# A one-core float32 kernel: loads at the start reordered, and the products of the first unit rearranged

## The reference, cut to what matters

```
xn   = rms_norm(x, gain)          # x: 256 x 2048; the row factor is 1/sqrt(mean(x*x)+eps)
proj = xn @ w_in                  # dv, fv, fg, dq, dk, fq, fk are column blocks of it
```

## Time and profile before

| what | value |
|---|---|
| median of 3 runs | 2824.51 us |
| the profiled execution | 2823.42 us, span 2821.6 us |
| TensorE busy | 2788.0 us, 99% of the span |
| VectorE / ScalarE / GpSimd busy | 65% / 50% / 24% |
| first product of TensorE starts at | 8.11 us |
| DMA, mean over the span | 198 GB/s |

### The profile page before, as it was taken

How to read it: one execution, slowest core, us unless ns; L and a number is a source line. 1 busy time by engine, 2 the same in 40 slices (tenths; PEclk the granted TensorE clock), 3 DMA queues, 4 the chain that set the end, 5 groups by cost and what they waited for, 6 DMA issues and landing times.

```text
span 2821.6 us, 39092 instructions
## 1 busy us (share of the span) xinstructions
PE 2788.0 (99%) x14972; PEld 2399.4 (85%) x14972; DVE 1824.2 (65%) x2904; ACT 1409.0 (50%) x1991; POOL 689.5 (24%) x365
## 2 busy tenths in 40 slices
PE   8999999999999999999999999999999999999998
PEld 6888888888888888888888888888888888999886
DVE  5566766877777755555555555656777876555554
ACT  5454644455555544454444444446655555444454
POOL 0000000388888888800000000001201111000000
PEclk9999999999999999999999999999999999999999
DMA  7653479877777777777677777765664556666664
GB/s 258 209 163 120 130 245 317 246 191 188 192 189 189 191 188 190 191 217 223 209 223 211 225 233 223 238 208 187 187 185 153 161 153 193 186 189 189 186 195 155
DMA packets 199018, 559.02 MB, mean 198 GB/s; under 512 B 53344, under 2 KB 69872, under 8 KB 195888
## 3 DMA queue, kind: packets, MB, share of 16 engines
q1 hardware_dynamic: 161456, 554.99, 63.5%
q0 software_dynamic: 36944, 0.41, 2.8%
q10 hardware_dynamic: 432, 1.12, 0.1%
HBM read 535.32 MB, written 21.12 MB: 197 GB/s over the span
## 4 chain that ended last, share of the span: by engine, by line
PE 92%; DVE 3%; ACT 2%; DMA 1%; issue 1%; POOL 0%; DVEq 0%; ACTq 0%; SPq 0%
PE bank L530 91%; DVE wlo L906 2%; ACT whi L1621 1%; PE bank L542 1%; DMA raw<-in_w_dv 1%; DMA h_scratch<-X 0%; DMA raw<-in_w_pq 0%; DVE tmpc L909 0%; ACT EB L1621 0%; ACT L1621 0%; DVE HB L909 0%; DVE QKb L909 0%; DVE AT L1160 0%; ACT scr L1621 0%; DVE EB L968 0%
## 5 line engine op out<-in xcount | busy, mean ns | idle before, releaser
L906 DVE TENSOR_TENSOR wlo<-raw,whi 128x1024 fp32r<-128x1024 f32 (+1 forms) x965 | 1188.9, 1234 | 864.3 <-ACT whi L1621 861.2
L1621 ACT ACTIVATE whi<-raw 128x1024 fp32r<-128x1024 f32 (+1 forms) x965 | 1017.2, 1056 | 1006.5 <-PE bank L530 985.9
L530 PE MATMUL bank<-aX,whi 128*128 128x512 f32 (+1 forms) x4000 | 966.9, 391 | 0.8 <-DVE aX L941 0.8
L530 PE MATMUL bank<-whi,aX 128*128 128x512 f32 x3008 | 934.1, 390 | 9.6 <-ACT whi L1621 9.1
L530 PEld LDWEIGHTS bank<-aX,whi 128*128 128x128 f32 (+1 forms) x4000 | 728.1, 188 | 142.9 <-issue 3.0
L530 PEld LDWEIGHTS bank<-whi,aX 128*128 128x128 f32 x3008 | 565.6, 188 | 129.1 <-ACT whi L1621 9.5
L1581 POOL DMA_INDIRECT gate_scratch<-gate,place x256 | 577.4, 2255 | 261.8 <-DMA gate_scratch<-HB 183.6
L530 PE MATMUL bank<-wlo,aX 128*128 128x512 f32 x1504 | 586.9, 390 | 3.2 <-DVE wlo L906 3.2
L530 PEld LDWEIGHTS bank<-aX,wlo 128*128 128x128 f32 (+1 forms) x3984 | 513.2, 191 | 22.6 <-DVE aX L941 2.1
L530 PE MATMUL bank<-aX,wlo 128*128 128x256 f32 (+1 forms) x3984 | 530.3, 283 | 1.8 <-DVE aX L941 1.7
L530 PEld LDWEIGHTS bank<-wlo,aX 128*128 128x128 f32 x1504 | 282.8, 188 | 64.3 <-DVE wlo L906 6.5
(11 more groups left out here) (227 smaller groups left out, 1821.6 us busy)
## 6 DMA issues: line engine op xcount, KB each, us to landing
raw<-in_w_down SPq DMA_DIRECT2D x256, 512.0 KB, 3.7
raw<-in_w_up SPq DMA_DIRECT2D x256, 512.0 KB, 4.2
raw<-in_w_in SPq DMA_DIRECT2D x176, 512.0 KB, 3.7
raw<-in_w_out SPq DMA_DIRECT2D x32, 512.0 KB, 4.3
gate_scratch<-HB SPq DMA_DIRECT2D x16, 1024.0 KB, 7.5
raw<-in_w_pq SPq DMA_DIRECT2D x32, 512.0 KB, 5.7
raw<-in_w_o SPq DMA_DIRECT2D x32, 512.0 KB, 4.3
raw<-in_w_pg SPq DMA_DIRECT2D x32, 512.0 KB, 4.3
```

The lines of the kernel that those rows point to most:

```text
L530: return e.matmul(o, lhsT, rhs, start=start, stop=stop, skip_group_check=True)
L906: e.tensor_tensor(wlo[:, s, 0:n], raw[:, r, 0:n], whi[:, s, 0:n].bitcast(F32), ALU.subtract).then_inc(s_lo, 1)
L1621: return e.activation(o, i, f, **k)
```

## The change

```
-    SQ0 = 1
-    ROWS0 = G["dv", 1].first
+    SQ0 = 6
+    ROWS0 = G["dv", 1].first + 4
@@ sync (DMA issue)
         for i, (a, z) in enumerate(XT_PARTS):
             e.dma_start(xT[:, a:z, :]..., I["xT"][:, a * 256:z * 256]).then_inc(s_xt[i], 16)
-        for u in range(2, NRAW):
-            load(u)
-        e.dma_start(small ...)
-        for t in range(2):
-            e.dma_start(X[:, t, :] ...).then_inc(s_x[t], 16)
-        e.dma_start(attc ...)
-        e.dma_start(fbr ...)
+            if i < NRAW:
+                load(i)
         for u in range(NRAW, NU + NRAW + NSPL):
             load(u)
+            if u == 6:
+                e.dma_start(small ...)
+                e.dma_start(X[:, 0, :] ...).then_inc(s_x[0], 16)
+            if u == 8:
+                e.dma_start(X[:, 1, :] ...).then_inc(s_x[1], 16)
+            if u == 11:
+                e.dma_start(attc ...)
+                e.dma_start(fbr ...)
@@ tensor
+        def first_unit():
+            bs = [vacant(fill) for fill in G["dv", 0].fills]
+            for high in (True, False):
+                for kt in range(2):
+                    c = slice(kt * 512, kt * 512 + 512)
+                    if high:
+                        w.wait_ge(s_hi if kt else s_h0, 1)
+                    else:
+                        w.wait_ge(s_lo, 1)
+                    w.wait_ge(s_xh, kt + 1)
+                    for t in range(2):
+                        ts = slice(t * 128, t * 128 + 128)
+                        if high:
+                            mm(bs[t], ax_hi(kt)[:, ts], whi[:, 0, c], kt == 0, False)
+                        else:
+                            last = mm(bs[t], ax_hi(kt)[:, ts], wlo[:, 0, c], False, False)
+                    if high:
+                        w.wait_ge(s_xl, kt + 1)
+                        for t in range(2):
+                            ts = slice(t * 128, t * 128 + 128)
+                            mm(bs[t], ax_lo(kt)[:, ts], whi[:, 0, c], False, False)
+            last.then_inc(s_mm, 1)
+            tick(0)
+
+        w.wait_ge(s_one, 1)
+        for _ in range(7):
+            mm(banks[7][:, 0:256], ones[:, 0:128], ones[:, 0:256], True, True)
+        first_unit()
+        group_t("dv", 0, ax_hi, ax_lo, split_x, 1)     # 1: skips unit 0
+        group_t("dv", 1, ax_hi, ax_lo, split_x)
@@ vector
-            if kt in (1, 3, 7):
+            if kt in (1, 3, 7, 11):
                 split((kt + 1) // 4 if kt > 1 else 0)
+        def values(name, i, base):                     # the same two evacuations of a group
+            ...
+        steps(G["dv", 0])
+        for u in G["dv", 1].units:
+            step(u)
+            if u == ROWS0 + 1:
+                values("dv", 0, 1024)
+        values("dv", 1, 1024)
+        for i in range(2):
+            steps(G["fv", i])
+            values("fv", i, 0)
@@ scalar
+            if u == SQ0 - 1:
+                warm()                                 # in step(u); was before step(0)
-        for u in range(2):
-            e.dma_start(raw[:, u, :], plan.src[u]).then_inc(s_raw[u], 16)
-            if kt in (1, 3, 7):
-                split((kt + 1) // 4 if kt > 1 else 0)
-        warm()
+            if kt == 1:
+                w.wait_ge(s_raw[0], 16)
+                act(whi[:, 0, 0:512], raw[:, 0, 0:512], ACT.Copy).then_inc(s_h0, 1)
+                act(whi[:, 0, 512:1024], raw[:, 0, 512:1024], ACT.Copy).then_inc(s_hi, 1)
+            if kt in (3, 7, 11):
+                split((kt + 1) // 4)
```

More of the change, by code:

```diff
@@ L152, in _build @@
     s_raw = [sem(f"s_raw{i}") for i in range(NRAW)]
-    s_hi, s_lo, s_mm, s_half = sem("s_hi"), sem("s_lo"), sem("s_mm"), sem("s_half")
+    s_h0, s_hi, s_lo, s_mm, s_half = sem("s_h0"), sem("s_hi"), sem("s_lo"), sem("s_mm"), sem("s_half")
     s_free = [sem(f"s_free{i}") for i in range(8)]
@@ L453, in _ @@
             e.dma_start(xT[:, a:z, :].rearrange("p k c -> p (k c)"), I["xT"][:, a * 256:z * 256]).then_inc(s_xt[i], 16)
-        for u in range(2, NRAW):
-            load(u)
-        e.dma_start(small[:, :], I["small"]).then_inc(s_const, 16)
-        for t in range(2):
-            e.dma_start(X[:, t, :], I["x"][:, t * D:t * D + D]).then_inc(s_x[t], 16)
-        e.dma_start(attc[:, :], I["att"]).then_inc(s_att, 16)
-        e.dma_start(fbr[:, :], I["forget_bias"]).then_inc(s_att, 16)
+            if i < NRAW:
+                load(i)
         for u in range(NRAW, NU + NRAW + NSPL):
             load(u)
+            if u == 6:
+                e.dma_start(small[:, :], I["small"]).then_inc(s_const, 16)
+                e.dma_start(X[:, 0, :], I["x"][:, 0:D]).then_inc(s_x[0], 16)
+            if u == 8:
+                e.dma_start(X[:, 1, :], I["x"][:, D:2 * D]).then_inc(s_x[1], 16)
+            if u == 11:
+                e.dma_start(attc[:, :], I["att"]).then_inc(s_att, 16)
+                e.dma_start(fbr[:, :], I["forget_bias"]).then_inc(s_att, 16)
             now = u - NRAW - NSPL + 1
@@ L721, in group_f, with group_t @@
                 tick(u)
-        def group_t(name, i, xh, xl, ready):
+        def group_t(name, i, xh, xl, ready, skip=0):
             g = G[name, i]
             bs = [vacant(fill) for fill in g.fills]
-            for u in g.units:
+            for u in g.units[skip:]:
                 s = u % NSPL
@@ L793, in split_x @@
             w.wait_ge(s_xl, kt + 1)
-        for name in ("dv", "fv"):
-            for i in range(2):
-                group_t(name, i, ax_hi, ax_lo, split_x)
+        def first_unit():
[28 more added lines that the diff above has]
+        for i in range(2):
+            group_t("fv", i, ax_hi, ax_lo, split_x)
         g = G["fg", 0]
@@ L1254, in step @@
                     low_two("ple", kp)
-            split(u + NSPL)
+            if u:
+                split(u + NSPL)
         def finish(x):
@@ L1352, in _ @@
                                    aX[:, kt, 0:256].bitcast(F32), ALU.mult, ALU.subtract).then_inc(s_xl, 1)
-            if kt in (1, 3, 7):
+            if kt in (1, 3, 7, 11):
                 split((kt + 1) // 4 if kt > 1 else 0)
[L1355 to L1365, removed]
+        def values(name, i, base):
+            g = G[name, i]
+            ready(g)
+            w.wait_ge(s_xl, 16)
+            w.wait_ge(s_rinv, 1)
+            for t in range(2):
+                b, _ = g.fills[t]
+                e.tensor_scalar(VV[:, t, base + i * 512:base + i * 512 + 512], banks[b], st[:, 24 + t:25 + t], None,
+                                ALU.mult).then_inc(s_free[b], 1)
+        steps(G["dv", 0])
[4 more added lines that the diff above has]
+        values("dv", 1, 1024)
+        for i in range(2):
+            steps(G["fv", i])
+            values("fv", i, 0)
         g = G["fg", 0]
```

## The result

22 runs of each kernel: 2818.68 us (2817.35 to 2822.99) after the change, 2823.36 us (2821.99 to 2825.76) before; ratio 0.9985, 95% interval 0.9979 to 0.9991. That is 4.7 us by the medians, 0.17%. By its own classes the result is "same", to which it gave 0.40, and not "faster", to which it gave 0.56. The profiled execution took 2819.23 us, span 2817.4.

The account below looks back on a forecast made before the run. TensorE, 99% busy, was held by start transfers until 24.9 us; its last early wait moves from 24.92 to 18.95, a 6.0 us gain, other edits nothing, so 2824.51 becomes 2818.5 us, range 2817.0 to 2823.0.

Parts of the forecast that it names:

- its own classes: Whole time: faster means a gain above 0.2%, 5.65 us, chance 0.56; same 0.40; slower 0.04.
- equivalent start: TensorE's last early wait less the work before it: 13.8 us before, 7.85 after, a gain of 6.0 us.
- The predicted covers: Slack at later units: table load 2.2 us, unit 7 behind x 2.0, unit 9 behind x's second half 2.4.
- the landings: Weight and input DMAs at the start: unit 0 at 6.1, unit 1 at 8.1, unit 4 at 15.9, 6.5 us earlier.
- the second product of unit 4 at 18.95 as the last wait: TensorE at the start: last early wait ends at 18.95 in place of 24.92, a gain of 6.0 us.
- The lag: Start transfers: a DMA lands 1.0 to 1.3 us after its bytes are through.
- the ones: Seven float32 products before unit 0 let it run at the fast level; had it run slow, equivalent start 9.2.
- whatever is gained by then reaches the end in full: After 24.9 us: TensorE's progress drives all later work, so the 6.0 us start gain reaches the end.
- Rival 1: Unit 0 lands no sooner, at 7.0 to 7.1: gain 5.0 us, 2819.5; chance 0.14.
- Rival 2 and 4: Rival 2: clock rises late, one or two units at 1.2 GHz, gain 4.6 or 2.2 (0.05); 4: held down, 2829.5 (0.04).
- Rival 3: x ahead of units 7 and 9 costs more than its 2.0 us cover: gain 4, 2820.5; chance 0.07.
- The prediction's last sign of being wrong: A start as forecast with the end not moved by as much: later work isn't driven by TensorE alone.

Follow-up runs that it names:

- x early: Changed kernel with small and both halves of x issued ahead of unit 4 again: 2825.93 us, ratio 1.0008.
- before with keys late: Kernel before the change, with the load of keys and SyncE's wait for the spill of h1 four units later: 2822.43 us, ratio 0.9996.
- high first 6 with keys late: Changed kernel with high products first in units 0 to 5, and keys and the spill wait four units later: 2816.01 us, ratio 0.9973.
- no ones: Changed kernel without the seven products of ones: 2818.59 us, ratio 0.9981.
- third cut late: Changed kernel with the cut of unit 3 after block 15 again and the table load ahead of it: 2824.60 us, ratio 1.0003.
- keys late: Changed kernel with the load of keys and SyncE's wait for the spill of h1 four units later: 2816.99 us, ratio 0.9977.
- high first 6: Changed kernel with high products first in units 0 to 5 instead of unit 0 alone: 2817.83 us, ratio 0.9979.
- the old order: Changed kernel with unit 0's twelve products in the old order: 2819.97 us, ratio 0.9986.
- ScalarE's queue: Changed kernel with units 0 and 1 issued by ScalarE's queue as before the change: 2820.57 us, ratio 0.9988.
- the zeros experiments: All 16 scratch-zeroing writes put before the pq units: kernel before 2824.35 us, changed kernel 2819.43, changed with high products first in units 0 to 5 2819.70.

## Why the prediction was right, and where it was not

**Luck in the number.** The time came out 0.2 us from the 2818.5 forecast, but two errors cancel there. The gain was forecast at 6.0 us and came at 4.7, 1.3 less; and the kernel before, 2824.51 in the three runs that the forecast started from, has 2823.36 over 22, 1.15 less.

**Confirmed.** TensorE's continuous stretch reaches back to the start, and what its equivalent start loses comes out at M1: 13.8 - 8.3 = 5.5 by the two starts, 5.44 found in the same pair of traces, and M1 less the equivalent start is 422.5 to 423.0 in all six traces of the two starts. The order of the loads carries it ("x early" costs 6.1 us), and so does the third cut with the table load (5.65). These two do not add up to the gain. Each alone is late enough to set TensorE's last early wait, which gives back 4.8 and 4.4 us, and the idling before that wait adds a slow stretch of 1.3 us. The predicted covers held: no wait between 11.24 and 120 us, with x ahead of units 7 and 9.

**Mis-sized: the landings.** With them went the second product of unit 4 at 18.95 as the last wait. Unit 0 landed at 5.7 (6.1 predicted), but part 1 at 7.5 (6.8), unit 1 at 8.8 (8.1) and part 2 at 10.0 (9.4). The lag between "its bytes are through" and "landed" had been taken from two queues, 1.0 to 1.3 us; in one queue unit 1's 1.64 MB are through at 7.0 (stretches above) and land 1.8 later. The last wait was therefore unit 1's, at 11.24, and VectorE's chain kept up behind it with little to spare: `wlo` of unit 4, begun at 18.26, is done at 19.5, where 18.9 was predicted; TensorE takes it up at 19.7. That cost 0.5 us in this trace. Over all ten traces with unit 1 in SyncE's queue it lands at 8.3 to 9.5, never at the 8.1 of the forecast, with a spread of 1.2 us that the forecast ("good to half a microsecond") did not have. In the two further traces of the new start, where it landed at 8.39 and 8.30, the equivalent start is 7.9 and 7.8, the forecast's 7.85, and the start gain of 5.8 at M1, the mean of the three pairs, is 0.2 us short of the 6.0.

**Mis-sized: the ones.** The prediction had the equivalent start at 9.2 without them, 1.35 us later than with them. The trace without them bears out the 9.2: unit 0 runs slow in all twelve products, 6.25 to 11.5, and the second product of unit 4 is at 20.31. But with them that product is at 19.71, 19.32 and 19.22, not at 18.95, so they bought 0.6 to 1.1 us there, 0.4 to 1.0 at M1, and nothing that the medians show.

**Wrong: "whatever is gained by then reaches the end in full".** The start alone was short by some 0.2 us, so by the medians most of the missing 1.3 us went here. The sentence held to M1 and from M2 on, but not between. Net of its idle time before S1, M1 to S1 is 25.95 to 25.97 us in the traces of before, changed, before with keys late, and high first 6 with keys late, and 27.56 or 27.57 in those of no ones, x early, third cut late, keys late and high first 6, which all have one stretch of 10 us at a granted clock of 0.83. So the stage has two costs, a wait for units behind the spill (0.3 to 2.7 us, 3.4 in the worst trace, at another place) and a fall of the clock (1.6 us) that comes in some executions and not in others (in those of the old order and of ScalarE's queue it came after S1: 26.09 and 26.03 to M2 in place of 24.48).

The wait has to be compared among traces without a fall before S1, since a fall, which slows TensorE, can hide part of it: there it is 1.40, 2.69, 2.64 and 1.85 us, and 0.31 in the two with keys late (with a fall it is 0.31 to 1.18 without the edit, 0.32 with it). So the order spill, keys, units is its cause; whether it is SyncE's standing still or the 1 MB of keys ahead of the units, the edit does not separate, since it moves both. That the changed kernel pays more of these costs on average (1.7 us over its version with keys late; before the change 0.9 to 1.3) is what the medians suggest, within their noise; why it should is open. It may be chance of the transfers: the loads behind the spill are issued 0.4 us sooner after M1 than before the change, yet the one that S1 waits for takes 1.71 us longer.

**Rivals.** Rival 1 (unit 0 no sooner) is out, 5.7 against 7.0; but its amount, a gain of 5.0, is near what came, by the later landing of unit 1. Rival 2 and 4 (clock late or held down) are out at the start: products of ones or none, TensorE was fast by 12.4. Their mechanism is real, though: it is what adds 1.3 us to each of the two undone parts. Rival 3 (x ahead of units 7 and 9) is out: no wait there. The prediction's last sign of being wrong, a start as forecast with the end not moved by as much, is the one that came, and no rival with a chance stood for it. The chances had 0.56 on more than 5.65 us; the start alone has 5.4 to 6.2, the whole 4.7.

## What to carry to other kernels

Express a start as the equivalent start of the bound engine (time of its last early wait, less the work before it): it can be compared across versions to a few tenths of a microsecond, and edits on other engines can be priced by it. Take it from more than one trace: here executions of the same kernel differ by 0.5 us in it, as much as the forecast missed by. When several suppliers are equally tight, undoing any one part takes nearly all of the gain away, so the value of a part is not its share. And before crediting a start gain to the end, list the later stages in which the bound engine waits for something that varies: a queue that stands still for one semaphore (here SyncE's, 10 us behind a spill) is such a place, and moving the waiting issue behind some loads that don't need it took the wait away, worth 0.9 to 1.7 us by the medians.

## What the runs showed of the hardware

After idle time of 2.53 + 0.84 us and of 3.36 + 0.83 us TensorE's products were up to 0.427 us apart (1.2 GHz) for 3.6 us (21.44 to 25.08, 24.54 to 28.18), where 1.02 + 0.83 us had left them at 0.227. Near M1, idle times of 1.19, 1.40 and 0.28 us within 5 us were followed by a stretch at a granted clock of 0.83 before S1 in five of eleven traces (the zeros experiments left aside), with the same code at that place; two more had it after S1, and four none. Each fall costs 1.6 us there.

Unit 1 landed between 8.3 and 9.5 us in ten traces that load it in the same order by one queue: a spread of 1.2 us for the same issues. The plain float32 product of 128 x 256 took 0.70 us in its place (seven in 4.87; 4.76 to 5.81 over nine other traces, 0.68 to 0.83 each), near the 0.74 worked out from the earlier trace rows for the slow level. The Trainium skill's "FP8 and Floating Point Precision" (TensorE precision notes) has four passes for it, an estimate of 0.85 at 1.2 GHz; the traces are 0.02 to 0.17 below.
